# Pitched activation tiles in a one-core transformer kernel on Trainium2

## What is computed

```python
def swiglu(h, w_gate, w_up, w_down):
    return (jax.nn.silu(h @ w_gate) * (h @ w_up)) @ w_down

def first_block(x, mem, ...):
    x = x + 0.5 * swiglu(rms_norm(x, ffn1_norm), ffn1_w_gate, ffn1_w_up, ffn1_w_down)
    x = x + token_mixing(rms_norm(x, mix_norm), w_in, ...)            # gated linear attention + conv
    x = x + memory_cross_attention(rms_norm(x, xattn_norm), rms_norm(mem, mem_norm), ...)
    x = x + 0.5 * swiglu(rms_norm(x, ffn2_norm), ffn2_w_gate, ffn2_w_up, ffn2_w_down)
    return rms_norm(x, final_norm)

def second_block(x, ...):
    x = diff_pool_layer(x, ...);  x = conv_glu_ffn(x, ...)   # differential attention + pooling
    x = swa_layer(x, ...);        x = conv_glu_ffn(x, ...)   # sliding-window attention
    return x
```

## Time and profile before

| | |
|---|---|
| median of 3 runs | 2379.6 us (2377.29 to 2385.77) |
| span of the profiled execution | 2377.1 us |
| outside the span, against the median | 2.5 us |
| TensorE busy | 2262.9 us, 95% |
| VectorE, ScalarE, GpSimd busy | 971.0, 849.1, 907.6 us |
| mean granted TensorE clock | 0.964 |
| HBM traffic | 207.05 MB read, 88 GB/s over the span |

### The profile page before, as it was taken

How to read it: one execution, slowest core, us unless ns; L and a number is a source line. 1 busy time by engine, 2 the same in 40 slices (tenths; PEclk the granted TensorE clock), 3 DMA queues, 4 the chain that set the end, 5 groups by cost and what they waited for, 6 DMA issues and landing times.

```text
span 2377.1 us, 29369 instructions
## 1 busy us (share of the span) xinstructions
PE 2262.9 (95%) x10442; PEld 1834.0 (77%) x10442; DVE 971.0 (41%) x1453; ACT 849.1 (36%) x1252; POOL 907.6 (38%) x383
## 2 busy tenths in 40 slices
PE   6999999999999999999979889999999879999998
PEld 5888887788787788888856668888888768888886
DVE  3222222454524522221234665555322985555421
ACT  4232222523433332222233534444322553444421
POOL 3444444332362344444422124444544104444442
PEclk8999999999999999999979879999999889999999
DMA  4333333122342233333322112333333103233332
GB/s 145 101 90 104 98 98 104 62 72 63 98 133 71 71 98 97 94 101 98 106 82 63 36 40 88 94 98 96 106 100 127 40 19 89 89 98 96 97 107 71
DMA packets 58687, 210.26 MB, mean 88 GB/s; under 512 B 6641, under 2 KB 7409, under 8 KB 58225
## 3 DMA queue, kind: packets, MB, share of 16 engines
q1 hardware_dynamic: 55584, 199.98, 27.4%
q10 hardware_dynamic: 3024, 9.19, 1.0%
HBM read 207.05 MB, written 2.10 MB: 88 GB/s over the span
## 4 chain that ended last, share of the span: by engine, by line
PE 73%; issue 14%; POOL 6%; DVE 6%; ACT 1%; POOLq 0%; ACTq 0%; DVEq 0%
PE psum L196 22%; PE psum L197 22%; PE psum L198 21%; POOL w_lo L170 6%; PE psum L214 1%; PE psum L216 1%; PE psum L215 1%; DVE swa_s L2019 1%; PE psum L1068 1%; PE psum L1093 1%; PE psum L652 1%; DVE swa_s L2037 1%; DVE swa_most L2025 0%; PE psum L648 0%; DVE swa_p_turned L2046 0%
## 5 line engine op out<-in xcount | busy, mean ns | idle before, releaser
L170 POOL TENSOR_TENSOR w_lo<-w_raw,w_hi 128x1024 fp32r<-128x1024 f32 x379 | 907.4, 2401 | 1445.2 <-ACT w_hi L158 1444.9
L196 PE MATMUL psum<-x_hi,w_hi 128*128 128x512 f32 x1808 | 724.7, 401 | 43.9 <-DVE x_lo L249 17.0
L197 PE MATMUL psum<-x_lo,w_hi 128*128 128x512 f32 x1808 | 716.4, 396 | 0.0
L198 PE MATMUL psum<-x_hi,w_lo 128*128 128x512 f32 x1808 | 715.7, 396 | 0.0
L158 ACT ACTIVATE w_hi<-w_raw 128x1024 fp32r<-128x1024 f32 x379 | 394.6, 1054 | 635.1 <-PE psum L198 596.5
L196 PEld LDWEIGHTS psum<-x_hi,w_hi 128*128 128x128 f32 x1808 | 346.8, 192 | 128.2 <-DVE x_lo L249 21.0
L198 PEld LDWEIGHTS psum<-x_hi,w_lo 128*128 128x128 f32 x1808 | 346.3, 192 | 75.1
L197 PEld LDWEIGHTS psum<-x_lo,w_hi 128*128 128x128 f32 x1808 | 347.1, 192 | 71.7 <-issue 0.2
L236 DVE SCALAR_TENSOR_TENSOR x<-psum,x 128x512 f32<-128x512 f32 x64 | 44.3, 692 | 396.4 <-PE psum L198 396.4
L249 DVE SCALAR_TENSOR_TENSOR x_lo<-x,columns,x_hi 128x512 fp32r<-128x512 f32 x64 | 118.3, 1849 | 69.4 <-ACT x_hi L267 69.4
L198 PE MATMUL psum<-ffn_hidden_hi,w_lo 128*128 128x512 f32 x352 | 138.7, 394 | 0.0
(11 more groups left out here) (286 smaller groups left out, 2621.3 us busy)
## 6 DMA issues: line engine op xcount, KB each, us to landing
w_raw<-in_stream SPq DMA_DIRECT2D x379, 512.0 KB, 3.6
swa_bias<-in_swa_bias ACTq DMA_DIRECT2D x1, 2048.0 KB, 8.6
out<-x ACTq DMA_DIRECT2D x8, 256.0 KB, 2.8
ab_bias<-in_ab_bias ACTq DMA_DIRECT2D x1, 1792.0 KB, 7.5
x<-in_x_in SPq DMA_DIRECT2D x4, 256.0 KB, 5.2
x<-in_x_in ACTq DMA_DIRECT2D x4, 256.0 KB, 6.6
xattn_mem<-in_mem ACTq DMA_DIRECT2D x1, 1024.0 KB, 5.0
mix_k_turned<-in_gate_w ACTq DMA_DIRECT2D x1, 256.0 KB, 3.5
```

Of the source, the lines that this page charges most:

```text
L170: pool.tensor_tensor(self.w_lo[:, split, :], self.w_raw[:, raw, :], self.w_hi[:, split, :].bitcast(F32), ALU.subtract).then_inc(self.w_lo_ ...
L196: pe.matmul(out, w_hi, hi[:, k0 + j, :], start=first and j == order[0], stop=False)
L197: pe.matmul(out, w_hi, lo[:, k0 + j, :], start=False, stop=False)
L198: mm = pe.matmul(out, w_lo, hi[:, k0 + j, :], start=False, stop=last and j == order[-1])
```

## The change

`x_hi` and `x_lo` get 16 floats (64 bytes) of gap behind each tile of 512, so tile k starts 2112 bytes after tile k-1 and not 2048. `x_lo` starts another 8 floats (32 bytes) into its buffer. The hidden buffers get 4 floats (16 bytes) of gap, a pitch of 2064 bytes, and the low one starts 4 floats (16 bytes) in. A new method `pitched` makes such a buffer and hands out the view of its tiles. The scratch for dynamic DMA is set to 4096 bytes instead of 16384, which makes room and moves everything behind it. The instructions of every engine stand in the same order with the same shapes as before.

```diff
-        self.x_hi = self.sb("x_hi", [P, DT, T], F32R)
-        self.x_lo = self.sb("x_lo", [P, DT, T], F32R)
+        self.x_hi = self.pitched("x_hi", DT, 16)
+        self.x_lo = self.pitched("x_lo", DT, 16, 8)
...
+    def pitched(self, name, tiles, gap, before=0, scope=None):
+
+        width = before + tiles * (T + gap)
+        buffer = (scope or self.ctx).enter_context(self.nc.sbuf_tensor(name, [P, width], F32R))
+        return buffer[:, before:width].rearrange("p (k t) -> p k t", t=T + gap)[:, :, 0:T]
...
-            self.h_hi = sb("hidden_hi", [P, FT, T], F32R)
-            self.h_lo = sb("hidden_lo", [P, FT, T], F32R)
+            self.h_hi = c.pitched(f"{name}_hidden_hi", FT, 4, 0, scope)
+            self.h_lo = c.pitched(f"{name}_hidden_lo", FT, 4, 4, scope)
...
-    nc = _bacc.Bacc("TRN2", target_bir_lowering=False, num_devices=1)
+    nc = _bacc.Bacc("TRN2", target_bir_lowering=False, num_devices=1, dynamic_dma_scratch_size=4096)
```

## The result

The changed kernel takes 2399.85 us (median of 4 runs, 2398.84 to 2401.42) against 2382.68 us (2377.29 to 2386.35) of the kernel before, whose 4 runs are the three given at the start and one more: ratio 1.0079, interval 1.0062 to 1.0097. The changed kernel is slower by 0.8%, where 2314 us was forecast. What came out is close to the 2399 us of the slower rival.

The account below looks back on a forecast made before the run. The prediction took TensorE's matmul starts to bound the kernel. Savings of 37 us (x) and 28 us (hidden), 65 us in all, taken from 2379.6 gave 2314 us, with a range of 2280 to 2403.

Parts of the forecast that it names:

- the slower rival: x's products never settle into their short step under changing residues: 230.0 ns, 19 us lost, 2399 us; chance 0.25.
- TensorE bounds the kernel and a step's change goes through one to one: TensorE is busy 95% of 2377.1 us and helpers wait for it, so matmul step changes reach the program's end.
- The place of both operands sets the step: Matmul steps: 226.7 ns with both operands at residue 128 of 512, 233 ns with 128 against 320.
- I take one step of 16 cycles (6.67 ns) below today's: 220.0 ns: x's 5616 products, pitched and offset, fall from 226.7 to 220.0 ns a step, saving 37 us.
- The bound from above: x's products at worst reach 233.3 ns, the worst settled step seen, 37 us lost over 5616 products.
- They are in the worse of the two placements seen, so nearly any other is more likely to be better: The hidden tiles' 2112 products, pitched, fall from 233.3 to 220.0 ns a step, saving 28 us.
- Mixed tiles at 0: 768 products on unpitched mixed tiles, moved from residue 320 to 352: 15 us saved to 5 us lost, taken as nothing.
- Writers and scratch at 0: ScalarE and VectorE writes of x and hidden tiles, and the 4096-byte scratch hiding weight landings, cost nothing.
- The rival of the lost settled step: Same as the slower rival: x's short step needs every tile and both parts at one residue; 2399 us, chance 0.25.
- The rule weighed: The skill's independent TensorE read ports for moving operand and weights would make the saving 0, the time 2380 us.

Follow-up runs that it names:

- the stages at 128: Kernel before plus small scratch and a 320-byte dummy putting hidden, mixed and memory tiles at the weights' residue 128; 2361.63 us, ratio 0.9927.
- the scans: Two unpitched kernels with small scratch, each stage's tiles moved a chosen distance from the weights' residue 128; one run each, 2372.96 and 2380.29 us.
- the x_lo offset: Kernel before with small scratch and x_lo alone starting 32 bytes further, no pitch; 2408.67 us against 2380.14, ratio 1.0116.
- the x part alone: Kernel before with small scratch and only the pitch and offset of x_hi and x_lo; 2411.98 us, ratio 1.0122.

## Why the prediction was wrong

- *TensorE bounds the kernel and a step's change goes through one to one.* Right: x's and the hidden products' steps account for 19.4 us, the span moved by 19.9; and for the stages at 128 the 6.6 ns x 2880 = 19 us came out as 17 us.
- *The place of both operands sets the step.* Right, and now shown by the stages at 128 and the scans. That the token products behave alike with the roles swapped is right for equal places alone.
- *"I take one step of 16 cycles (6.67 ns) below today's: 220.0 ns"* for x. This is the step that failed. Measured 231.2 ns: instead of 37 us saved, 24 us lost. The reason given, that equal residues which still pay 32 cycles read like a collision of two streams, turned the evidence around. The trace of before had the two placements side by side, and the equal one was the shorter. Equal places are the best of the twelve distances modulo 256 that were measured, so moving x away from them lost. The bound from above (233.3 ns, 37 us) held for x, though 233.3 ns is not the worst settled step there is: 4 bytes give 238.0.
- *"They are in the worse of the two placements seen, so nearly any other is more likely to be better"* for the hidden tiles. The sign was right and the size was not: 231.8 ns and 3 us, where 220.0 ns and 28 us were taken. A pitch of 16 bytes goes through all multiples of 16 in turn; the eleven of them that the runs have average 232.0 ns, and the tiles got 231.8. What would have given the gain is distance 0: 226.7 ns, 14 us.
- *Mixed tiles at 0.* Right: 233.3 ns before and after, since distances 192 and 224 cost the same.
- *Writers and scratch at 0.* Right: x_lo 1854 ns, ratio 1.0006 for the scratch alone.
- *The rival of the lost settled step* had the right place, nearly the right price (230.0 ns, 2399 us) and, with 0.25, the second highest chance. Its mechanism was half right. A settled state does exist for x and is lost, and the x_lo offset shows that one unequal matmul in three loses it for its neighbours. But sameness from tile to tile is not what it needs: the hidden tiles had that, and ran at 233.3 ns. That its 2399 us was met within 1 us is in part luck: x lost 24 us where it had 19, and the hidden products gained 3 where it had none.
- *The rule weighed.* The Trainium skill (SBUF — State Buffer, "Who interferes with whom") has TensorE's two read ports as independent. The measurement decides against it as far as time goes: with nothing changed but a dummy of 320 bytes (the scratch alone changes no step) the step moves by 6.6 ns, up to 11.3 ns over the scans.

A check of the theory on the changed kernel itself: x_hi's tiles stand at distances 0, 64, 128, 192 and x_lo's at 32, 96, 160, 224, twice over. By the scans (224 by the mixed tiles of the changed kernel, 233.3 ns) the averages are 230.6 and 233.6 ns, and two parts of the first to one of the second give 231.6; measured 231.2. For the pitch of 64 without offset the same sum gives 230.6 against 231.8, and for the x_lo offset 228.9 against 232.7 over all stages. So the table gives the direction and rough size where placements change from matmul to matmul, not the exact step.

**Open.** Why equal places still pay 12.9 ns over the 213.8 of the earlier trace rows, how neighbouring matmuls affect each other, and why the pattern repeats at 256 bytes. All weight pieces had one residue, so no run tells whether a moving tile's distance counts to its own weights or to those of the next matmul, which are loaded meanwhile. Pitched or shifted weights against unshifted ones, and a w_lo at another place than w_hi, were not tried.

## What to carry to other kernels

Where a kernel is bound by a stream of float32r matmuls, compare the distance between matmul starts of stages that do the same work: the durations in the profile show only part of it (389 against 394 ns for the hidden products at 128 and before, where the steps differ by 6.6), the starts show all. Where the products are 128x512, lay the moving tiles and the weight pieces out so that they start at the same address modulo 256 bytes, which a dummy buffer of a few hundred bytes can do; it was worth 0.7 to 0.9% here. For other widths measure it: the 256-wide products of this kernel were slightly slower that way. And before a layout is changed to avoid a supposed collision, look at which of the layouts already in the trace is the fast one.

## What the runs showed of the hardware that was not expected

- The step of a 128x512 float32r matmul at the full clock depends on the distance of the two operands' start addresses modulo 256 bytes: 226.7 ns at 0, 228.9 at 64, 231.1 to 234.3 at the other multiples of 16 that were measured, 238.0 at 4 bytes. On the last the Trainium skill (SBUF — State Buffer, "Door 1: The DMA port swizzle", the remark on cachelines) says that SBUF has lines of 16 bytes and that each crossing to a new one costs; only the 4-byte start is off such a line here, and it is the slowest, which agrees in direction; one distance can't show that this is the cause. That page has nothing on the distance between operands.
- One operand in three at another place (x_lo by 32 bytes) takes the short step from all three: 233.3 ns in three of the feed-forward stages and 231.7 in the fourth, 232.7 over all.
- The width matters: with equal places the 256-wide products with the memory's activations take 119.4 ns on average, against 117.3 in the kernel before. The 128-wide token products with x take 111.6 to 111.7 ns both before and after the change.
- The same kernel can get one stretch more at the lower TensorE clock in some executions: the x part alone ran at 2412 to 2414 us in three of four runs and at 2398.33 in one, and in its profile swa's input projection had a stretch of 20.5 us at 1.2 GHz that the changed kernel ran at 2.4 GHz, after the same work and the same pause of TensorE.
